# A 16-column gate group of a projection moved from the channel-stationary part into the last token-stationary group, and turned by TensorE

## The reference

```python
h = _rms(x, P['norm_mix_pre'])
proj = jnp.einsum('btd,dc->btc', h, P['w_in'])
hq, hf, hi, hg, rw, sq, sk, sv, gq, gk, gv, ga, gg = _split(proj, IN_WIDTHS)
...
log_a = jax.nn.log_sigmoid(ga.astype(F32) @ a2.astype(F32) + a_b.astype(F32)) / GLA_GATE_NORM
...
o = _rms(o, norm_w) * jax.nn.silu(heads(gg.astype(F32)))
```

## Time and profile before

| | us |
|---|---|
| median of 3 runs | 1910.58 |
| the runs | 1910.0, 1918.42, 1910.58 |
| the profiled execution | 1910.01 |
| its span, first to last instruction | 1908.4 |
| TensorE busy | 1738.1 |
| ScalarE busy | 782.5 |
| VectorE busy | 1014.3 |

### The profile page before, as it was taken

One profiled execution on the slowest core, in us unless ns is written; L12 is line 12 of the kernel. 1 busy time (PEld: TensorE's weight loads), 2 busy tenths in 40 slices (PEclk: granted clock), 3 DMA queues, 4 the chain that ended last, 5 costly groups with the idle time before them and its releaser, 6 DMA issues.

```text
span 1908.4 us, 32727 instructions
## 1 busy us (share of the span) xinstructions
PE 1738.1 (91%) x13007; PEld 1390.0 (73%) x13007; DVE 1014.3 (53%) x1678; ACT 782.5 (41%) x1655; POOL 366.1 (19%) x600
## 2 busy tenths in 40 slices
PE   5999999999875789868888799899999999999997
PEld 5999989944444667458887344688888878888785
DVE  7211111066255766463442155866666655668988
ACT  3111111165454645632332132555555543546664
POOL 4600021188434465610011100000000000000000
PEclk9999999999887665579996899999999999999998
DMA  6211131120262010100000522243344386655874
GB/s 164 56 45 35 45 97 54 46 64 1 86 195 75 25 29 27 30 1 3 2 2 1 178 77 83 65 146 122 122 143 151 109 293 214 197 169 185 291 249 177
DMA packets 157020, 193.37 MB, mean 101 GB/s; under 512 B 21443, under 2 KB 95827, under 8 KB 156867
## 3 DMA queue, kind: packets, MB, share of 16 engines
q1 hardware_dynamic: 143842, 171.87, 28.3%
q0 software_dynamic: 7296, 19.21, 3.3%
q10 hardware_dynamic: 5728, 0.19, 0.2%
HBM read 144.76 MB, written 46.46 MB: 100 GB/s over the span
## 4 chain that ended last, share of the span: by engine, by line
PE 48%; DVE 4%; ACT 2%; issue 1%; DMA 1%; SPq 0%; POOL 0%; DVEq 0%; ACTq 0%
PE ps L2587 6%; PE ps L3191 5%; PE ps L3192 5%; PE ps L3193 5%; PE ps L2722 5%; PE ps L2724 5%; PE ps L2723 5%; PE ps L2732 1%; PE ps L2117 1%; PE ps L2138 1%; PE ps L2134 1%; PE ps L2041 1%; PE ps L3177 1%; PE ps L3178 1%; PE ps L2190 0%
## 5 line engine op out<-in xcount | busy, mean ns | idle before, releaser
L3191 PE MATMUL ps<-dn_form 128*128 128x512 f32 x448 | 175.9, 393 | 5.7 <-DVE dn_form L3120 3.2
L3192 PE MATMUL ps<-dn_form 128*128 128x512 f32 x448 | 175.6, 392 | 0.0
L3193 PE MATMUL ps<-dn_form 128*128 128x512 f32 x448 | 175.3, 391 | 0.0
L3120 DVE TENSOR_TENSOR dn_form<-arena,dn_form 128x1024 fp32r<-128x1024 f32 x112 | 137.0, 1223 | 71.7 <-ACT dn_form L3115 69.4
L3115 ACT ACTIVATE dn_form<-arena 128x1024 fp32r<-128x1024 f32 x112 | 118.6, 1060 | 135.4 <-PE ps L3193 91.9
L3376 POOL DMA_DIRECT2D out_y_prompt<-arena x4 | 2.2, 551 | 816.9 <-DVE arena L3317 816.9
L447 PE MATMUL ps<-h_hi,w_split 128*128 128x384 f32 (+3 forms) x432 | 142.3, 329 | 2.6 <-POOL h_lo L406 2.6
L479 DVE CAST w_split<-w_raw 128x1024 fp32r<-128x1024 f32 (+1 forms) x28 | 19.4, 692 | 235.0 <-PE ps L449 235.0
L449 PE MATMUL ps<-h_hi,w_split 128*128 128x384 f32 (+3 forms) x432 | 141.7, 328 | 0.0
L448 PE MATMUL ps<-h_lo,w_split 128*128 128x384 f32 (+3 forms) x432 | 141.6, 328 | 0.0
L2587 PE MATMUL ps<-arena 128*128 128x512 f32 (+1 forms) x288 | 127.9, 602 | 8.7 <-DMA arena<-in_w_out 8.7
(11 more groups left out here) (453 smaller groups left out, 4214.5 us busy)
## 6 DMA issues: line engine op xcount, KB each, us to landing
arena<-in_w_down SPq DMA_DIRECT2D x160, 256.0 KB, 3.6
u_scratch<-arena SPq DMA_DIRECT2D x112, 256.0 KB, 2.8
arena<-u_scratch SPq DMA_DIRECT2D x112, 256.0 KB, 3.6
arena<-in_w_up SPq DMA_DIRECT2D x32, 512.0 KB, 6.0
w_raw<-in_w_in SPq DMA_DIRECT2D x27, 512.0 KB, 3.8
arena<-in_x_prompt SPq DMA_DIRECT2D x16, 512.0 KB, 3.8
arena<-in_cache_sb_k SPq DMA_DIRECT2D x64, 128.0 KB, 2.7
arena<-in_cache_sb_v POOLq DMA_DIRECT2D x64, 128.0 KB, 2.8
```

The costliest lines, as they stand in the source:

```text
L3120: dve.tensor_tensor(df[n % NDF][:, 1, :, :], sides(n), df[n % NDF][:, 0, :, :].bitcast(F32), ALU.subtract)\
L3191: pe.matmul(out, a_hi, b_hi, start=(j == 0), stop=False, skip_group_check=True)
L3192: pe.matmul(out, a_hi, b_lo, start=False, stop=False, skip_group_check=True)
L3193: ins = pe.matmul(out, a_lo, b_hi, start=False, stop=(j == NCH - 1), skip_group_check=True)
```

## The change

`ga` leaves the list of T units, which leaves 17, and gets its own small load (`ga_raw`, on SP's queue ahead of the weight units that `project_sync` loads). The split of the two `gg` units also splits 8 `ga` columns each into eight extra columns of each weight slot, which are now 136 wide (`WCOLS`). The nine `gg` tiles move 2 x 136 columns in place of 2 x 128. ScalarE evicts each of these tiles in two parts, the 256 columns with Silu and the 16 with Copy, into a staging tile that is 16 columns wider. TensorE turns the 16 columns of a tile with one transpose (`ga_turn`) two tiles later; the last two turns come behind the ninth tile. ScalarE copies the turned columns to `gaT` in three parts (`ga_evict`): one after tile 6, two after all jobs. `sb_tensor` waits for all three. The staging ring shrinks to 4 tiles.

```diff
-            ("hf", 256), ("gq", 128), ("gk", 128), ("ga", 16))
+            ("hf", 256), ("gq", 128), ("gk", 128))
...
-STAGES = 5
+STAGES = 4
+GA = 16
+WCOLS = P + GA // 2
...
-            return u % WSLOTS
+            return (u + len(T_UNITS) % 2) % WSLOTS
...
-            dve.tensor_copy(w_hi, raw).then_inc(S("w1_hi"), 1)
+            ins = dve.tensor_copy(w_hi, raw)
+            if name == "gg":
+                dve.wait_ge(S("ga_in"), 16)
+                g_raw = ga_raw[:, :, GA // 2 * a:GA // 2 * (a + 1)]
+                g_hi, g_lo = (w1[:, y, w_slot(u), :, P:WCOLS] for y in range(2))
+                ins = dve.tensor_copy(g_hi, g_raw)
+            ins.then_inc(S("w1_hi"), 1)
...
+            if name == "gg":
+                ins = dve.tensor_tensor(g_lo, g_raw, g_hi.bitcast(F32), ALU.subtract)
...
         def project_sync(sp):
+            sp.dma_start(ga_raw[:, :, :], A["w_in"][0].rearrange("(k p) c -> p k c", p=P)[:, :, COL["ga"]:COL["ga"] + GA])\
+                .then_inc(S("ga_in"), 16)
...
+                cw = WCOLS if name == "gg" else P
+                w_hi, w_lo = (w1[:, y, w_slot(u):w_slot(u) + 2, :, 0:cw] for y in range(2))
                 for i in range(NT):
                     r = rows(i)
                     pe.wait_ge(S("proj_out"), n - PBANKS + 1)
-                    out = ps[0:r, P_BANKS[n % PBANKS], 0:GW].rearrange("p (a c) -> p a c", a=2)
+                    if name == "gg" and i >= 2:
+                        ga_turn(pe, i - 2)
+                    out = ps[0:r, P_BANKS[n % PBANKS], 0:2 * cw].rearrange("p (a c) -> p a c", a=2)
...
+            for i in (NT - 2, NT - 1):
+                ga_turn(pe, i)
+
+        def ga_stage(i):
+
+            return stage[0:rows(i), (len(JOBS) - NTJ - NT + i) % STAGES, GW:GW + GA]
+
+        def ga_turn(pe, i):
+            pe.wait_ge(S("proj_out"), len(JOBS) - NT + i + 1)
+            if i == NT - 1:
+                pe.wait_ge(S("ga_out"), 1)
+            c = i % 4 * P
+            pe.transpose(ps[0:GA, 1 + i // 4 % 2, c:c + rows(i)], ga_stage(i), ident[0:rows(i), 0:rows(i)])\
+                .then_inc(S("ga_turn"), 1)
+
+        def ga_evict(act, n):
+
+            act.wait_ge(S("ga_turn"), min(4 * n + 4, NT))
+            tw = min(512, TOK - 512 * n)
+            act.activation(gaT[0:GA, 512 * n:512 * n + tw], ps[0:GA, 1 + n % 2, 0:tw], ACT.Copy)\
+                .then_inc(S("ga_out"), 1)
...
+                    if name == "gg":
+                        if a >= STAGES:
+                            act.wait_ge(S("ga_turn"), a - STAGES + 1)
+                        src = bank[0:r, 0:2 * WCOLS].rearrange("p (a c) -> p a c", a=2)
+                        act.activation(stage[0:r, m % STAGES, 0:GW].rearrange("p (a c) -> p a c", a=2),
+                                       src[:, :, 0:P], fn)
+                        act.activation(ga_stage(a).rearrange("p (a c) -> p a c", a=2), src[:, :, P:WCOLS], ACT.Copy)\
+                            .then_inc(S("proj_out"), 1)
+                        if a == 6:
+                            ga_evict(act, 0)
+                        continue
...
+            for n in (1, 2):
+                ga_evict(act, n)
...
         def sb_tensor(pe):
             pe.wait_ge(S("proj_out"), len(JOBS))
+            pe.wait_ge(S("ga_out"), 3)
```

More of the change, by code:

```diff
@@ L94, in build @@
                    "u_out1": ("d_k1", 512), "q_in0": ("la_s0", 128), "q_in1": ("x_in2", 48), "q_in2": ("w_out_b", 16),
-                   "x1_in": ("sv_in", 32), "y_early": ("stage0", 176), "up_sum": ("d_sum", 9), "up_lo": ("d_q", 6), "up_snap": ("d_zr", 9),
+                   "x1_in": ("sv_in", 32), "y_early": ("stage0", 224), "up_sum": ("d_sum", 9), "up_lo": ("d_q", 6), "up_snap": ("d_zr", 9),
                    "up_c": ("d_z", 9), "up_c21": ("d_o", 4), "u_sq": ("d_kT", 32), "u_smp": ("sb_l", 33),
                    "t_sum": ("sb_zc", 33), "t_hi": ("sb_w", 33), "t_lo": ("sb_sp", 33), "q_sum": ("sb_spm", 17),
-                   "q_hi": ("sb_o", 4), "q_lo": ("w1_split", 28), "q_ps": ("sb_pv", 33), "z_hi": ("proj_out", 108),
-                   "z_lo": ("w1_hi", 28), "y_ps": ("sb_x", 57), "y_copy": ("h_hi", 18), "y_add": ("h_tmp", 18),
+                   "q_hi": ("sb_o", 4), "q_lo": ("w1_split", 27), "q_ps": ("sb_pv", 33), "z_hi": ("proj_out", 105),
+                   "z_lo": ("w1_hi", 27), "y_ps": ("sb_x", 57), "y_copy": ("h_hi", 18), "y_add": ("h_tmp", 18),
                    "y_fold": ("sb_z", 33), "y_half": ("d_zt", 9), "q_in3": ("x_in0", 128), "q_in4": ("x_in1", 112),
@@ L203, in build @@
             h_tmp = place.enter_context(nc.sbuf_tensor("h_tmp", [P, 2, 4, P], F32))
-            place.enter_context(nc.sbuf_tensor("below_h_lo", [P, LO - H_TMP - 8 * P], F32))
+            place.enter_context(nc.sbuf_tensor("below_ga_raw", [P, NR - TOK - H_TMP - 8 * P], F32))
+            ga_raw = place.enter_context(nc.sbuf_tensor("ga_raw", [P, KD, GA], F32))
+            place.enter_context(nc.sbuf_tensor("below_h_lo", [P, LO - NR + TOK - KD * GA], F32))
             h_lo = place.enter_context(nc.sbuf_tensor("h_lo", [P, KD, TOK], F32R))
-            w1 = place.enter_context(nc.sbuf_tensor("w1_split", [P, 2, WSLOTS, KD, P], F32R))
+            w1 = place.enter_context(nc.sbuf_tensor("w1_split", [P, 2, WSLOTS, KD, WCOLS], F32R))
             w1_raw = place.enter_context(nc.sbuf_tensor("w1_raw", [P, RSLOTS, KD * P], F32))
-            stage = place.enter_context(nc.sbuf_tensor("nat_stage", [P, STAGES, GW], F32))
+            stage = place.enter_context(nc.sbuf_tensor("nat_stage", [P, STAGES, GW + GA], F32))
         nat_scratch = nc.dram_tensor("nat_scratch", [4, TOK, GW], F32, kind="Internal").ap()
@@ L526, in project_tensor @@
                 pe.wait_ge(S("w1_split"), u + 2)
-                w_hi, w_lo = (w1[:, y, w_slot(u):w_slot(u) + 2, :, :] for y in range(2))
+                cw = WCOLS if name == "gg" else P
+                w_hi, w_lo = (w1[:, y, w_slot(u):w_slot(u) + 2, :, 0:cw] for y in range(2))
                 for i in range(NT):
@@ L550, in project_act @@
                         act.wait_ge(S(f"stage{m % STAGES}"), 16 * (m // STAGES))
-                    act.activation(stage[0:r, m % STAGES, :], bank[0:r, 0:256], fn).then_inc(S("proj_out"), 1)
+                    if name == "gg":
[9 more added lines that the diff above has]
+                        continue
+                    act.activation(stage[0:r, m % STAGES, 0:GW], bank[0:r, 0:256], fn).then_inc(S("proj_out"), 1)
                     continue
                 t0, tw = EG[tg]
-                cw = 16 if name == "ga" else P
-                src = bank[0:cw, 0:tw]
+                src = bank[:, 0:tw]
                 if name in ("rr", "rk", "rv", "rx"):
@@ L565, in project_act @@
                     dst = (gqT if name == "gq" else gkT)[:, t0:t0 + tw]
-                elif name == "ga":
-                    dst = gaT[0:cw, t0:t0 + tw]
                 else:
@@ L600, in stage_out_gpsimd @@
                     dst = nat_scratch[NAT.index(name), i * P:i * P + r, :]
-                pool.dma_start(dst, stage[0:r, m % STAGES, :]).then_inc(S(f"stage{m % STAGES}"), 16)
+                pool.dma_start(dst, stage[0:r, m % STAGES, 0:GW]).then_inc(S(f"stage{m % STAGES}"), 16)
         def nat_in_sync(sp):
```

3 lines of the change are left out of this document (2 added, 1 removed).

## The result

The changed kernel takes 1903.92 us in the median, the kernel before 1911.42 us beside it; the ratio is 0.9954 with a 95% interval of 0.994 to 0.9967. That is a gain of 8.8 us (6.3 to 11.5), where 8.1 us were forecast, and the median lies in the forecast range of 1898.5 to 1907.0. The ratio leaves out one slow execution of each kernel (3718.41 and 6970.5 us); the medians, which count them, are 7.5 us apart. The profiled execution took 1898.99 us against 1910.01, and its span is 1897.4 us against 1908.4, so that one pair shows 11.0 us.

What follows compares the result with a forecast made beforehand. TensorE's matmuls were taken to bound the projection, with ScalarE's work also on the path at the hand-offs. 11.91 - 1.45 - 1.33 - 1.02 = 8.11 us off 1910.01 gave 1901.9 us; range 1898.5 to 1907.0.

Steps and rivals of the forecast that it cites:

- The unit that goes: Channel-stationary part: removing the 72 ga matmuls takes 11.91 us from TensorE's path; the hand-off behind them stays the same.
- VectorE's copies now write a strided tile: Weight splits into the wider slots: the stride does not take VectorE's fast pace away, so no cost.
- The extra columns: gg group: 216 matmuls move 272 columns in place of 256, costing 1.45 us (0 to 5.8).
- Rival (b): gg matmuls: the extra columns cost a fixed amount, 4.4 us more than counted, 1906.3 us; chance 4%.
- The turns: Seven single transposes between gg tiles: 0.19 us each (0.099 plus 0.09 for the change back), 1.33 us (0.5 to 3.9).
- Rival (a): Transposes between gg tiles: the pipeline empties at each, 2.6 us less gain, 1904.5 us; chance 12%.
- The end of the projection: Last projection matmul to scores: ScalarE's extra eviction and copies delay scores and table load alike by 1.02 us (0.8 to 1.9).
- The ring: Staging tiles, 4 in place of 5: costs nothing, with 0.6 and 1.1 us of cover in the v group.
- The weight slots: Wider slots for the gate columns: cost nothing, judged by VectorE's strided writes and its free time.
- (c): Stages behind the projection: an earlier start gets a better clock, up to 3.4 us per window, hence 1898.5 us; chance 18%.
- (d): Stages behind the projection: an earlier start gets a worse clock, 17 us over five windows, 1919 us; chance 6%.
- Rival (e): Whole change: it doesn't do what it says, as the path goes to weights or staging; given no chance of its own.

## Why the prediction held, point by point

**What bounds the kernel.** Right, for the projection: the runs without and with twice the ga unit move the whole by 11.3 us one way and the other.

**The unit that goes.** 11.57 us measured, 11.91 forecast. The unit was sized right, but the 17 that stay became slower (0.85 us in the run with slots of 136 alone), and the matmul stream does not start at the same time in every run: ScalarE's first eviction of 384 columns behind 90 us comes at 90.92 to 91.49 us in twelve of the fourteen traces, at 91.47 in before and 91.00 in after. -11.91 + 0.85 - 0.47 = -11.53 us is nearly all of it. The step that failed is "VectorE's copies now write a strided tile", which looked only at who writes the slots; TensorE reads them too.

**The extra columns.** 1.45 us forecast, 1.62 between the runs with 272 and 256 columns. The forecast took the window of 26.00 us for the length of the group, which is 25.66 and a step of 0.12 us; with that a column costs 0.43 ns and the term is 1.49 us. Rival (b), a fixed price of 5.8 us, is dead.

**The turns.** 1.33 us forecast, 7 x 0.11 = 0.77 measured, and again 0.11 for each of 14 more. The mis-sized term is the 0.099 us for the transpose itself; the 0.09 us for the change back is right (a step of 0.21 us behind the turn where 0.12 is usual), and beside it only 0.02 us are seen. Rival (a), emptying at each turn, is dead for the seven turns of 128 rows, whose stationary width goes from 128 to 16 and back. The rule of the Trainium skill that I weighed there (TensorEngine Tiling (Array Packing), Key Properties: a change of tiling mode drains TensorE) may show in this kernel, but with the rows and not with the columns: the ninth turn uses 64 of 128 rows and costs 0.35 us, and with all rows in use 0.11. That the 0.35 us are such a draining is a reading of the gaps; what the runs show is the time and the rows. The load of the 64-row turn is not pulled ahead either. On that, the Trainium skill, TensorE: Matmul & The Clock Gate, section "Step-by-step: what each phase is for", says that the queue pulls weight loads ahead where row groups don't conflict or the background buffer is the target; the traces agree for 128 rows (0.12 us ahead) and show no pull for 64 rows behind 128 (0.00 us).

**The end of the projection.** 1.02 us forecast, 0.70 measured. I added full durations of ScalarE's operations, and they overlap: from start to start the 16 columns take 0.06 us where I had 0.2, and the copy of 512 takes 0.48 where I had 0.60. The other 0.06 us are the eviction ahead of them and the copy of 64, which overlap too. That scores and table load shift alike was right (371.48 and 371.40). With gg ahead of gv this term is gone, as the gap of 0.74 us shows, but the turns that it covered are then paid.

**What was to cost nothing.** The ring: right, 131.47 us in both. The weight slots: wrong in sign and kind. The wider pitch gives 1.15 us in the N part and takes 0.85 us in the units, and nothing in my rows spoke of either.

**The sum.** 8.11 us to the first score became 9.69. The 1.58 us are 0.95 from the four groups between, 0.65 within gg (0.56 from the turns and 0.24 from the pitch, as in the other groups, less 0.17 on the columns, and 0.02 of rounding) and 0.32 from the end, less 0.34 in the unit part. That 8.8 us in the whole run lie so near the forecast of 8.1 is in part luck: to the first score the forecast missed 1.58 us, and the interval of 6.3 to 11.5 us holds both sums. The range was said to take in the forecast with its ends; it leaves out the upper end of the terms, 1909.7 us.

**Rivals (c) and (d).** Behind the first score 9 us of spread go along with the granted clock, and whole runs of both kernels spread by 14 and 16 us. No median moved by it beyond the intervals, so on this comparison it can't be told from noise; that a start some 10 us earlier costs a microsecond or so behind the scores, the way of (d), is not ruled out either. The profiled execution, 11.0 us faster, would alone have looked like (c); the ratio does not. Rival (e) is dead by the two runs with none and two ga units.

## What to carry to other kernels

A matmul group with few stationary columns costs what its moving columns cost; and it can pay to make its columns moving columns of another group, here 11.9 us against 1.6 for the columns, 0.8 for the turns and 0.7 for the hand-off. A lone transpose between matmuls cost 0.11 us here while it kept the number of rows in use and 0.35 where it did not, so try padding a short last tile to full rows where the extra results can be ignored. And when a tile's pitch changes, look at every engine that reads it: a price for the writer says nothing of TensorE's pace.

## What the runs showed of the hardware that was not expected

- The pitch of weight blocks changed TensorE's pace by 0.6 to 3%, one way or the other: from 128 to 136 words, 24 matmuls moving 2 x 128 columns from them take 2.84 in place of 2.88 us with 128 stationary tokens, and 2.81 in place of 2.73 with 64; with the same blocks stationary, 72 matmuls take 11.93 in place of 11.86, though in two runs blocks of 128 took 11.90. The distance between slots, 1024 or 1088 words, changed nothing with blocks of 128.
- A transpose of 16 or of 128 columns between matmuls costs the same 0.11 us; one that goes from 128 rows to 64 and back costs 0.35, and its weight load is not begun ahead of it.
- ScalarE's records overlap by 0.10 us where nothing is waited for between them: the next starts 0.28 us into a record of 0.38, and 0.06 us into one of 0.16.
